# All eight up units of a chunk in seven block products, their weight sums on GpSimd, and a ring whose low part lies over the raw weights

## The reference

```python
h = rms_norm(x, norm_ffn)
x = x + (jax.nn.silu(h @ w_gate) * (h @ w_up)) @ w_down      # w_gate, w_up: 2048 x 5632; w_down: 5632 x 2048
return rms_norm(x, norm_final)
```

## Time and profile before

| | |
|---|---|
| median of 3 runs | 1362.46 us |
| the profiled execution, its own time | 1363.83 us |
| its span in the profile | 1362.1 us |
| TensorE, VectorE, ScalarE, GpSimd busy | 1350.7, 950.6, 712.1, 44.8 us |
| read from HBM | 257.33 MB, 190 GB/s over the span |

### The profile page before, as it was taken

One profiled execution on the slowest core, in us unless ns is written; L12 is line 12 of the kernel. 1 busy time (PEld: TensorE's weight loads), 2 busy tenths in 40 slices (PEclk: granted clock), 3 DMA queues, 4 the chain that ended last, 5 costly groups with the idle time before them and its releaser, 6 DMA issues.

```text
span 1362.1 us, 26444 instructions
## 1 busy us (share of the span) xinstructions
PE 1350.7 (99%) x11247; PEld 1315.9 (97%) x11247; DVE 950.6 (70%) x1241; ACT 712.1 (52%) x927; POOL 44.8 (3%) x70
## 2 busy tenths in 40 slices
PE   8999999999999999999999999999999999999997
PEld 7888999999999999999999999999999999999997
DVE  6554456667654756767899899985546899988554
ACT  6333356656545664455655655544344555555444
POOL 3000010000000110000000000000000000000111
PEclk9999999999999999999999999999999999999999
DMA  7776555544565667555566666656556666666653
GB/s 244 248 229 223 181 170 156 155 140 141 156 188 167 194 204 225 182 187 171 185 194 197 220 195 190 198 197 208 199 189 189 196 214 191 194 192 230 211 194 124
DMA packets 135264, 261.08 MB, mean 192 GB/s; under 512 B 8448, under 2 KB 25408, under 8 KB 134768
## 3 DMA queue, kind: packets, MB, share of 16 engines
q1 hardware_dynamic: 132912, 251.13, 57.8%
q0 software_dynamic: 1792, 7.57, 1.6%
q10 hardware_dynamic: 448, 0.76, 0.2%
HBM read 257.33 MB, written 2.10 MB: 190 GB/s over the span
## 4 chain that ended last, share of the span: by engine, by line
PE 98%; DMA 1%; DVE 0%; ACT 0%; issue 0%; ACTq 0%; DVEq 0%
PE bank L649 26%; PE bank L651 25%; PE bank L650 25%; PE bank L888 5%; PE bank L891 5%; PE bank L890 5%; PE bank L637 3%; PE bank L787 1%; PE bank L698 1%; DMA raw_ring<-in_w_in 0%; DMA sigmoid_gates<-in_norm_mix 0%; PE bank L747 0%; PE bank L1011 0%; PE bank L699 0%; PE bank L835 0%; PE bank L813 0%
## 5 line engine op out<-in xcount | busy, mean ns | idle before, releaser
L1327 DVE TENSOR_TENSOR weight_lo_ring<-raw_ring,weight_hi_ring 128x1024 fp32r<-128x1024 f32 (+2 forms) x479 | 582.3, 1221 | 317.9 <-ACT weight_hi_ring L1071 260.4
L1071 ACT ACTIVATE weight_hi_ring<-raw_ring 128x1024 fp32r<-128x1024 f32 (+2 forms) x431 | 450.6, 1050 | 459.3 <-PE bank L651 299.5
L649 PE MATMUL bank<-weight_hi_ring,hT_hi 128*128 128x256 f32 (+2 forms) x1276 | 380.9, 298 | 0.0
L651 PE MATMUL bank<-weight_hi_ring,hT_lo 128*128 128x256 f32 (+2 forms) x1276 | 375.5, 294 | 0.0
L650 PE MATMUL bank<-weight_lo_ring,hT_hi 128*128 128x256 f32 (+2 forms) x1276 | 375.5, 294 | 0.0
L649 PEld LDWEIGHTS bank<-weight_hi_ring,hT_hi 128*128 128x128 f32 x1276 | 239.8, 188 | 10.0 <-issue 3.4
L650 PEld LDWEIGHTS bank<-weight_lo_ring,hT_hi 128*128 128x128 f32 x1276 | 239.9, 188 | 6.1
L651 PEld LDWEIGHTS bank<-weight_hi_ring,hT_lo 128*128 128x128 f32 x1276 | 239.6, 188 | 6.3
L649 PE MATMUL bank<-weight_hi_ring,h2T_hi 128*128 128x256 f32 x704 | 195.5, 278 | 0.0
L650 PE MATMUL bank<-weight_lo_ring,h2T_hi 128*128 128x256 f32 x704 | 194.6, 276 | 0.0
L651 PE MATMUL bank<-weight_hi_ring,h2T_lo 128*128 128x256 f32 x704 | 194.6, 276 | 0.0
(11 more groups left out here) (253 smaller groups left out, 1933.5 us busy)
## 6 DMA issues: line engine op xcount, KB each, us to landing
raw_ring<-in_w_in SPq DMA_DIRECT2D x96, 512.0 KB, 3.5
raw_ring<-in_w_gate SPq DMA_DIRECT2D x88, 512.0 KB, 4.3
raw_ring<-in_w_up SPq DMA_DIRECT2D x88, 512.0 KB, 4.2
raw_ring<-in_w_down SPq DMA_DIRECT2D x88, 512.0 KB, 4.0
raw_ring<-in_w_in SPq DMA_DIRECT2D x55, 480.0 KB, 4.2
raw_ring<-in_w_out SPq DMA_DIRECT2D x32, 512.0 KB, 4.0
raw_ring<-in_w_br_c SPq DMA_DIRECT2D x16, 256.0 KB, 3.8
raw_ring<-in_w_br_a SPq DMA_DIRECT2D x16, 256.0 KB, 6.5
```

The lines of the kernel that those rows point to most:

```text
L649: pe.matmul(dst, x_hi, w_hi, start=opening, stop=False, skip_group_check=True)
L651: m = pe.matmul(dst, x_lo, w_hi, start=False, stop=last and k == UK - 1, skip_group_check=True)
L1071: act.activation(whi[:, s, :, 0:width(u)], raw[:, s, :, 0:width(u)], ACT.Copy)\
L1327: dve.tensor_tensor(lo, w, hi.bitcast(F32), ALU.subtract).then_inc(lo_ready, 1)
```

## The change

SEVEN becomes all eight up units, so that the branch for the others goes. The three sums move from VectorE to GpSimd, with three buffers in place of one. The low part of a unit is written over its raw weights: the raw and low rings are one ring of six slots, the high ring has five, and the space won holds a buffer of sums. A load now waits until TensorE has used unit u-6, and ScalarE's split until it has used u-5. High parts of the sums have three buffers; each low part is written over its sums. Three loops of the first projection are written out. `up_rows` loses half an addition, the order of units within a chunk is moved by a place or two, and the sums of the activations are made for two more groups.

```diff
-RING = 4
+RING = 6
+HI_RING = 5
+EXT = 3
+KEPT = 4
-SEVEN = (0, 1, 2, 4, 5, 7)
+SEVEN = tuple(range(8))
-            plan += g[0:5] if i == a else [last[4], g[0], g[1], g[2], last[5], last[6], last[7], g[3], g[4]]
-            plan += [up[0], g[5], g[6], up[1], g[7], up[2], up[3]]
+            plan += g[0:6] if i == a else [g[0], last[4], g[1], last[5], g[2], last[6], last[7], g[3], g[4], g[5]]
+            plan += [up[0], g[6], up[1], g[7], up[2], up[3]]
...
+        raw_at = top[0]
         raw = place("raw_ring", [RING, UK, W])
-        wlo = place("weight_lo_ring", [RING, UK, W], F32R)
+        wlo = at("weight_lo_ring", [RING, UK, W], raw_at, F32R)
...
+            t_sum = [at(f"weight_sums{e}", [3, Q4], a) for e, a in enumerate(low_places)]
...
             def free(count):
-                sp.wait_ge(lo_ready, count)
+                sp.wait_ge(unit_used, count)
...
@@ the loop over SEVENS stands on GpSimd, between its load of x (line 620) and the wait at line 623
+            for n, u in enumerate(SEVENS):
+                t = t_sum[n % EXT]
+                quarter = raw[:, u % RING, :, :].rearrange("p k (c n) -> p (k c) n", c=2)
+                pool.wait_ge(raw_ready[u % RING], landed(u))
+                if n >= EXT:
+                    pool.wait_ge(unit_used, SEVENS[n - EXT] + 1)
+                link(pool, "pool", pool.tensor_tensor(t[:, 0:2, :], quarter[:, 1:2, :].to_broadcast([P, 2, Q4]),
+                                                      quarter[:, 0:4:3, :], ALU.subtract))
+                link(pool, "pool", pool.tensor_tensor(quarter[:, 1, :], quarter[:, 0, :], t[:, 1, :], ALU.subtract))
+                pool.tensor_tensor(t[:, 2, :], quarter[:, 2, :], quarter[:, 1, :], ALU.subtract).then_inc(w_summed, 1)
...
-                if not is_seven(u):
-                    for k in range(UK):
-                        into(i, 3, 0, block(k, 0), quarters(u, k, 0), stop)
...
@@ ScalarE
             def split(u):
-                if u >= RING:
-                    act.wait_ge(unit_used, u - RING + 1)
+                if u >= HI_RING:
+                    act.wait_ge(unit_used, u - HI_RING + 1)
...
@@ VectorE
-            def sums_of_weights(u):
...
             def split(u):
-                if is_seven(u + 1) and not is_seven(u):
-                    sums_of_weights(u + 1)
-                split_unit(u % RING, u + 1, width(u))
+                split_unit(u, width(u))
                 if is_seven(u):
...
-                if is_seven(u + 1) and is_seven(u):
-                    sums_of_weights(u + 1)
...
-                dve.tensor_tensor(quarter[:, 0:4:3, :], three, p_sb[:, :, :], ALU.add).then_inc(up_emptied, 1)
+                dve.tensor_tensor(quarter[:, 0, :], three[:, 0, :], p_sb[:, 0, :], ALU.add).then_inc(up_emptied, 1)
```

More of the change, by code:

```diff
@@ L251, in place @@
             return t
+        raw_at = top[0]
         raw = place("raw_ring", [RING, UK, W])
-        whi = place("weight_hi_ring", [RING, UK, W], F32R)
-        wlo = place("weight_lo_ring", [RING, UK, W], F32R)
+        whi = place("weight_hi_ring", [HI_RING, UK, W], F32R)
+        spare_at = top[0]
+        top[0] = spare_at + 4 * UK * W
+        wlo = at("weight_lo_ring", [RING, UK, W], raw_at, F32R)
         ident = place("identity", [P])
@@ L326, in build_layer @@
         ext_at = mid + 8 * KD * S + (MOVING - STATIONARY) % LINE
-        ext_hi = at("weight_sums_hi", [2, 3, Q4], ext_at, F32R)
-        ext_lo = at("weight_sums_lo", [2, 3, Q4], ext_at + 2 * 3 * 4 * Q4, F32R)
-        assert ext_at + 4 * 3 * 4 * Q4 <= nc.sbuf_top
+        n_sum = 3 * 4 * Q4
+        ext_hi = at("weight_sums_hi", [EXT, 3, Q4], ext_at, F32R)
+        low_places = (ext_at + EXT * n_sum, span[0] + (MOVING - span[0]) % LINE, spare_at)
+        assert low_places[0] + n_sum <= nc.sbuf_top and low_places[1] + n_sum <= mid
+        ext_lo = [at(f"weight_sums_lo{e}", [3, Q4], a, F32R) for e, a in enumerate(low_places)]
+        t_sum = [at(f"weight_sums{e}", [3, Q4], a) for e, a in enumerate(low_places)]
         h_sb = at("h2_two_blocks", [2, 2, P], low + 8 * KD * S)
@@ L505, in xload @@
                 sp.dma_start(X[:, :, cols], x_b[:, :, cols]).then_inc(x_ready[n], 16)
-            for n in range(RING):
+            for n in range(len(X_PIECES)):
                 xload(n)
-                if n > 0:
+                if 0 < n < len(X_PIECES) - 1:
                     straight(n)
[L511 to L522, removed]
+            for u in range(len(X_PIECES) - 1, U_FFN):
                 straight(u)
@@ L637, in transpose, with products @@
                 return pe.transpose(dst, src, ident[0:n, 0:n])
-            def products(slot, lhs, pair, first, last, k0, width=W, tiles=tuple(range(TT)), halves=(0, 1), apart=False):
+            def products(u, lhs, pair, first, last, k0, width=W, tiles=tuple(range(TT)), halves=(0, 1), apart=False):
                 l_hi, l_lo = lhs
@@ L893, in quarters @@
             def quarters(u, k, c):
-                return tuple(m[:, u % RING, k, c * Q4:(c + 1) * Q4] for m in (whi, wlo))
+                cols = slice(c * Q4, (c + 1) * Q4)
+                return whi[:, u % HI_RING, k, cols], wlo[:, u % RING, k, cols]
             def up_unit(u, i, j):
@@ L917, in extra @@
                 def extra(r):
-                    return tuple(m[:, e, r, :] for m in (ext_hi, ext_lo))
+                    return ext_hi[:, e, r, :], ext_lo[e][:, r, :]
                 into(i, 6, 0, block(0, 0), quarters(u, 0, 0), True)
@@ L974, in finishing @@
                 def finishing(t, halves):
-                    for j in range(n - RING, n):
+                    for j in range(n - KEPT, n):
                         u = AT["down", LAST_DOWN, j]
@@ L1037, in _ @@
                     m.then_inc(gains_full, 1)
[L1038 to L1049, removed]
+            for u in range(UPC, U_FFN):
                 straight(u)
@@ L1070, in split @@
                     act.wait_ge(raw_ready[s], landed(u))
-                act.activation(whi[:, s, :, 0:width(u)], raw[:, s, :, 0:width(u)], ACT.Copy)\
+                act.activation(whi[:, u % HI_RING, :, 0:width(u)], raw[:, s, :, 0:width(u)], ACT.Copy)\
                    .then_inc(hi_ready, 2 if u == 1 else 1)
@@ L1074, in split @@
                     n = N_SEVEN[u]
[L1075 to L1084, removed]
+                    act.activation(ext_hi[:, n % EXT, :, :], t_sum[n % EXT][:, :, :], ACT.Copy).then_inc(ext_hi_ready, 1)
             def hi_of_transposed(n, b, dst, gain):
@@ L1278, in _ @@
             root(1)
[L1279 to L1282, removed]
+            for u in range(UPC, U_END + LAG):
                 if u < U_END:
@@ L1381, in up_rows @@
                 chain(dve.tensor_tensor(u_four[:, :, :], seven, u_two[:, :].unsqueeze(1).to_broadcast([P, 2, Q4]), ALU.add))
-                dve.tensor_tensor(p_sb[:, 1, :], seven[:, 0, :], u_four[:, 1, :], ALU.add)
-                chain(dve.tensor_tensor(quarter[:, 1:3, :], two, u_four[:, :, :], ALU.add))
-                dve.tensor_tensor(quarter[:, 0:4:3, :], three, p_sb[:, :, :], ALU.add).then_inc(up_emptied, 1)
+                dve.tensor_tensor(quarter[:, 3, :], seven[:, 0, :], u_four[:, 1, :], ALU.add)
+                dve.tensor_tensor(quarter[:, 1:3, :], two, u_four[:, :, :], ALU.add)
+                dve.tensor_tensor(quarter[:, 0, :], three[:, 0, :], p_sb[:, 0, :], ALU.add).then_inc(up_emptied, 1)
                 dve.wait_ge(up_emptied, i + 1)
@@ L1712, in _ @@
             dve.wait_ge(rstd_ready, 1)
[L1713 to L1719, removed]
-                            empty_projection(c, bass.ds(i * (2 * WQ) + c * WQ, WQ))
             dve.wait_ge(consts_ready, 1)
             dve.wait_ge(sinks_ready, 16)
-            for u in range(U_MIX - UPC, U_END + LAG):
+            for u in range(UPC, U_END + LAG):
                 if u < U_END:
```

39 lines of the change are left out of this document (13 added, 26 removed).

## The result

The changed kernel takes 1405.78 us in the median of four runs (1403.03 to 1407.59) against 1362.41: 1.0312 times as long (interval 1.03 to 1.0325), 43 us slower. The profiled execution took 1403.03 us, 39.2 more than the one before. The prediction had slower, 1394 us, range 1368 to 1428.

The account below looks back on a forecast made before the run. TensorE was taken to bound the kernel, VectorE close behind at 92%. Sum: -4 (first stretches) + 34.4 (chunks, saving included) + 1 (start) = +31.4 on the median 1362.46, about 1394 us, slower by 2.3%; range 1368 to 1428.

Parts of the forecast that it names:

- The exclusion: Feed-forward chunks: VectorE instructions with two SBUF inputs and GpSimd's SBUF reads never overlap; GpSimd's part is 2.41 us per unit.
- The chunk: Feed-forward part: one chunk takes 45.5 us instead of 42.37, ends 44.8 and 48, adding 34.4 us over 11 chunks.
- the stepping: One round of the new order stepped: 3.3 us of stalls, G0 wanted at 24.8, ready 26.8; ends at 45.1.
- The floor of 44.8: Per chunk, shared time of VectorE and GpSimd summed, against TensorE's 41.7 us; operations reading PSUM (3.6 us) left out.
- the signs that the prediction named: Feed-forward: TensorE idle 3 to 4 us per chunk, marks 45 to 46 apart, L1327 1.5 to 1.7 us, 66 matmuls fewer.
- The saving: Two more up units per chunk lose three matmuls each: 0.68 us per chunk, 7.5 us over 11 chunks.
- each half begins with gate units and a full lead, so its first stretch stalls less: minus 2 us each: First stretch of each feed-forward half: a full lead of the ring takes off 2 us each, ends 0 and 9.
- The start: Last chunk of the first projection, units 248 wide: the new ring's shorter lead costs 1 us, ends 0 and 3.
- covered: In-place low part and six slots: loads start five units before use, leaving 7 us after load and splits; no cost elsewhere.
- The first (sums hidden, faster): Feed-forward chunks: GpSimd's sums and VectorE's low parts share time, saving counts in full, 1356 us; chance 9%.
- The second (lead swallows the floor): Exclusion holds, but only the floor counts and each half's lead swallows 9 us: 1372 us; chance 9%.
- The third, the turnaround: A unit's way through six slots is the limit: 17.4 us, 46.4 per chunk, 48 with slower hand-overs, 1421 us; chance 15%.

Follow-up runs that it names:

- p8_write_long: Changed kernel with GpSimd's three sums per unit replaced by four memsets in a row, which write SBUF but read nothing: 1360.19 us, 0.9973 of the kernel before.
- the short one: Changed kernel with GpSimd's three sums per unit replaced by one memset of 768 columns: 1357.40 us, 0.9955 of the kernel before.
- v6_new_rings: Changed kernel's rings, order and written-out loops with the old assignment, six units of seven products and sums on VectorE: 1368.14 us, 1.0033 of the kernel before.
- v7: Changed kernel with seven units of seven products per chunk (all but index 6), sums on VectorE: 1399.16 us, 1.0249 of the kernel before.
- old7: Kernel before with seven units of seven products, changed unit order, two buffers of sums, next sums made earlier: 1384.96 us, 1.0123 computed with the runs.
- p8_two: Changed kernel with GpSimd's middle operation of 256 columns left out, two of three per unit: 1376.69 us, 1.0086 of the kernel before.
- v8: Changed kernel with the three sums of all eight up units back on VectorE, GpSimd idle: 1401.57 us, 1.0271 of the kernel before.

## Why the prediction was right

**The exclusion** carried it, and it is shown: alternation in the trace after, and the whole loss gone when GpSimd writes without reading (p8_write_long). By the Trainium skill's page "SBUF — State Buffer", section "Who interferes with whom", a GpSimd instruction that only writes SBUF is not in VectorE's way; the 1222 ns of L1304 in p8_write_long agree. The operation of 256 columns, which no row of before showed, was put at 0.72 us alone and is 0.74 at 846.87.

**The chunk** was stepped to 45.1 and taken as 45.5; measured 45.8. The largest stall stands where the stepping put it, at the G0 behind U3, by the same chain. The floor of 44.8 left out VectorE's 3.6 us of PSUM operations, under which GpSimd may have nothing to do; the chunk lies a third of the way into them. That they do not exclude agrees with the unchanged 677 ns of L1359 and with the pair at 845.48. Of the signs that the prediction named, the marks (45.8 us apart in the mean), the 66 matmuls and the long 256-column operations (1476 and 1338 ns in the mean) came as said. The low part's mean was put at 1.5 to 1.7 us and is 1.78 in the window above. TensorE's idle time was put at 3 to 4 us per chunk. Its rows show 2.3 (4.65 in the window), all ending at L1306 except for rounding; by the marks the stall is 45.8 - 41.7 = 4.1, since a matmul's row is longer than its pace and covers part of a stall.

**The saving** of 7.5 us was right: intervals of 41.7 us in p8_write_long. Only 3 to 6 us of it are in that and the short one's medians, because 1.1 us are lost at the start and 1.6 in the first stretch, which comes next: 7.5 - 2.7 = 4.8, and its profiled execution is 4.8 us below that of the kernel before.

**What was mis-sized.** First, "each half begins with gate units and a full lead, so its first stretch stalls less: minus 2 us each". From 588.46 to 711.3 are 122.8 us; TensorE's content is the 121.9 of before less 2 x 0.34 and the 2.38 of U0, 118.8: 4.0 of stall, and 4.3 in the second half by the same working. So a first stretch loses as much as every other chunk, and the 4 us come back. In the second half this is the exclusion: the marks across it are 176.5 us apart here and 172.2 in p8_write_long. In the first half only part of it is. From the first transposes of x to the first mark are 123.0 us here (588.3 to 711.3) and 120.6 in p8_write_long (588.2 to 708.8), where GpSimd reads nothing; so 1.6 of the 4.0 us have another cause. They are lost around 668, behind the low part of a unit that VectorE makes only after the norm's statistics and low parts of the activations' sums. v6_new_rings, with the old number of those sums, loses 1.2 there (120.9 us against 122.1 less 2.38), so it is the rings or the order of units, for which the prediction had 0 there. Which of them is open. Second, 0.3 us per chunk, 3.7 in all. Together 8 us: predicted +31.4, measured +39.2 on the profiled executions. Third, the offset to the median: the profiled execution was the fastest of the four. They took 1403.03, 1404.35, 1407.22 and 1407.59 us at mean granted clocks of 0.998, 0.999, 0.995 and 0.996, and the prediction held the clock to be untouched. The clock alone does not order them, since 1404.35 ran at the highest.

**The start**: +1 predicted, 1.1 found, and at the place that it named, behind the last chunk of the first projection: TensorE waits 1.4 us at 174.1 for VectorE (L1444), where it waited 0.3 before. But "covered" for the in-place low part and the six slots was too simple: v6_new_rings is 4.7 us slower than the kernel before beside it. In the profiled executions the difference is 3.2 us (1367.00 and 1363.83): 0.3 before the feed-forward part, the 1.2 of the first stretch and 1.5 in its interval of 43.9 us. What delays that interval was not followed up.

**The rivals.** The first (sums hidden, faster) is out: the shared time stayed at 45.8. The second (lead swallows the floor) is out by the stalls of the first stretches. The third, the turnaround, is not the limit at six slots (seven bring nothing, and four high slots alone cost nothing), but is at five. As it was put, 17.4 us over six slots, it came within 0.6 us of the measured interval for another reason.

## What to carry to other kernels

In these runs work given to GpSimd was free for VectorE only where GpSimd's instruction read no SBUF, or VectorE's had at most one input there. Before moving it, add GpSimd's reading time to VectorE's time on operations with two SBUF inputs; if the sum is more than the bounding engine needs, it is the new bound, and here 2.41 us of exclusion replaced 1.6 us of own work. A second engine at over 90% is not a margin: in three versions (v7, old7, p8_two) a budget that fitted on paper (41.3 of 42.0, twice, and 39.8 of 41.7) left 1.6 us or more of stall per chunk.

## What the runs showed of the hardware that was not expected

TensorE's clock falls after stalls of about 2 us, in some executions of these kernels. Three windows of v7, 10 us each, columns as in the earlier trace rows:

```profile
760.00:770.00 10.00, 9.58 (x85) 9.39 (x83) 8.62 (x13) 5.90 (x8) 0.00 (x0) 1.00 0.70 207
770.00:780.00 10.00, 7.84 (x55) 7.67 (x54) 9.76 (x14) 5.85 (x8) 0.00 (x0) 0.83 0.37 110
780.00:790.00 10.00, 10.00 (x88) 10.00 (x86) 8.97 (x10) 5.01 (x6) 0.00 (x0) 1.00 0.67 205
```

TensorE stood idle for 2.2 of the middle 10 us, and the mean granted clock there is 0.83: a third of the window at the lower of its two levels, 1.2 of 2.4 GHz, worth 1.7 us of TensorE's time. Five such drops stand in v7's profiled execution, six in v8's feed-forward part, none in the feed-forward part of the changed kernel, whose longest wait was 2.0 us. So a stall of this size can cost TensorE nearly its own length again. Whether the kernel pays it depends on the limit: in v8's chunks VectorE was busy or waiting for ScalarE throughout, so the drops there need have added nothing. The executions of v7 spread from 1386.72 to 1405.24 us, where those of the kernel before spread by 3. Clock is only part of that: from a mean of 0.999 to 0.995 are 0.004 of 1400 us, some 6 us by this working, of 18.5. The rest is open.
